# Two-block transformer on one core: rope angles on GpSimd, two more weight places, another order of small steps

## The chip, the cores and the metric

One Trainium2 chip, one core. The metric is the device time of one execution in microseconds (us), the median over runs. All data is f32. TensorE is PE in the rows, VectorE DVE, ScalarE ACT, GpSimd POOL, SyncE SP. A "q" behind a name is the engine's queue that issues a DMA.

## The reference

Two blocks of two layers each, on x of 256 tokens by 1024. Cut to what matters here:

```python
def first_block(...):
    for i in range(DEPTH):                       # DEPTH = 2
        u = h @ w_in[i]
        y_mla, y_diff, y_sb = ...                # three attentions: MLA, differential, stick-breaking
        mix = jnp.concatenate([y_mla, y_diff, y_sb], axis=-1) @ w_o[i]
        h = layer_norm(DEEPNORM_ALPHA * h + mix, ln1_g[i], ln1_b[i])
        ffn = grouped_moe(h, ...)                # 16 experts of width 512, top 2
        ple = jax.nn.sigmoid(h @ ple_gate[i]) * (p[i] @ ple_proj[i])
        h = layer_norm(DEEPNORM_ALPHA * h + ffn + ple, ln2_g[i], ln2_b[i])

def second_block(...):
    for l in range(DEPTH):
        proj = x @ w_in[l]
        a = gla_branch(...) @ w_branch[0]
        b = gmlp_branch(...) @ w_branch[1]
        c = moba_branch(...) @ w_branch[2]       # softmax attention with a partial rope
        ga, gb, gc = split(sigmoid(gl), 3)
        mix = (ga * a + gb * b + gc * c) @ w_out[l]
        x = layer_norm_2(ALPHA * x + mix, ...)
        x = layer_norm_2(ALPHA * x + jnp.square(jax.nn.relu(x @ w_ff1[l])) @ w_ff2[l], ...)
```

Rope tables are cos and sin of position times frequency, with one set of frequencies for each block.

## The kernel before, in words

**Weights.** Every large weight is cut into units of 1 MB (128 partitions by 2048 f32). `weight_plan` lists them in the order of use; SyncE loads them in that order (line 454) into numbered places, each as soon as the place's former unit has been used. A dense unit lies in one of three raw places and is split before use: ScalarE writes a rounded high part (`split_scalar`, line 461, two halves of 128x1024), VectorE the rest (`split_vector`, line 468, two halves). TensorE multiplies high by high, high by low and low by high (lines 488, 489, 492 for results with channels on partitions, 496, 499, 500 for results in rows). There are NSPLIT = 3 places for split units. The call `feed(name)` on ScalarE and on VectorE, at the point of the engine's program where it is written, splits all units up to two behind `name`; `split_scalar` first waits until TensorE has used the unit three before (`former_split`).

**Experts.** Each of the first block's layers has 96 expert units (16 experts, 6 each: gate, up, down), used whole, from 16 places: the raw and split places and parts of the arena that are free at the time. `assign_places` gives each unit the place that comes free first among those allowed; near the end of a layer fewer are allowed (the dense units that follow need theirs). Rows of tokens are picked for each expert (line 1619 multiplies them).

**Order.** Each engine runs its own program, in order, written by hand with semaphore waits. PSUM's eight banks are taken in turn (`banks.take`) or by number (`banks.hold`), each behind the engine that emptied it before.

**The first output projection.** In `block1` TensorE makes the prefix products of stick-breaking (lines 1128 to 1137), the MLA scores (line 679), turns the differential attention's rows (line 515), makes stick-breaking's y (lines 663, 664: 8 heads' products) and then runs w_o in four units of 256 rows, in the order 1, 2, 3, 0, turning MLA's probabilities and making its y between. Before these, VectorE scales the diff rows: variance (line 1436, behind ScalarE's squares of line 780), rsqrt on GpSimd (line 775), product (lines 1457, 1459); it subtracts the prefix products for stick-breaking in between (line 1451), and ScalarE takes the exponential of the result (line 1298).

**Tables.** During layer 0, steps of a generator are put between the others: the rope angles on VectorE (lines 902 to 915, 16 instructions of 128x256 for each block), sines on ScalarE (line 870), the relative bias by buckets (lines 938, 980, 878, stored and loaded again by the DMAs of lines 879 and 888, masked at line 953). GpSimd copies the up-weights (lines 1495 to 1498) and is nearly unused otherwise.

**The mix stage** of the second block: MoBA's scores (line 679) and softmax (lines 2384, 2403, 797), twelve gate units "branch gate ihj" (sigmoid at line 2158) and six branch units "branch ih", in the order gate 000, 001, 010, 011, branch 00, 01, gate 100 and so on. Behind branch 01 TensorE turns MoBA's probabilities (line 515), which ScalarE and VectorE copy (lines 2156, 809); gMLP's y is split for branch 1 (`opb_hi`, line 702, and `opb_lo`, line 705); VectorE multiplies the branch's product with the gate in two halves (line 2421).

## Time and profile before

| | us |
|---|---|
| median of 3 runs | 1705.57 (1703.49 to 1705.96) |
| the profiled execution | 1704.55 |
| its span | 1703.3 |
| TensorE busy | 1645.7 (97%) |
| VectorE busy | 890.1 (52%) |
| ScalarE busy | 716.9 (42%) |
| GpSimd busy | 33.0 (2%) |
| mean granted TensorE clock | 0.991 |
| DMA | 413.11 MB, mean 243 GB/s |

Times in the rows are in us from the span's start. A timeline row gives start, duration, engine, line, operation, what is written and read, and how many instructions run together; the brackets at its end hold the idle time before it and whose work ended it. A granted clock of 1.00 is 2.4 GHz, 0.50 is 1.2 GHz.

### The profile page before, as it was taken

Reading aid. Unit: us, or ns where it says so; the run is one execution under the profiler, and the core shown is the slowest. Engines: PE = TensorE matmul, PEld = TensorE weight load, DVE = VectorE, ACT = ScalarE, POOL = GpSimd, SP = SyncE. Lnnn points to the kernel's source line nnn. Section 1 sums busy time; section 2 is a strip of 40 time slices with the busy share of each in tenths; the row PEclk is TensorE's granted clock in tenths of the full one; section 3 lists DMA queues with packets and bytes.
Section 4 is the critical chain, followed back from the end, with each engine's and each line's share of the span. In section 5 each row is a group of like instructions: output and inputs, shape, how many; then the busy total and the mean of one; then the engine's idle time right before and its main releaser. Section 6 shows DMA issues by size and latency. Waiting matters only on the chain.

```text
span 1703.3 us, 25713 instructions
## 1 busy us (share of the span) xinstructions
PE 1645.7 (97%) x10980; PEld 1287.6 (76%) x10980; DVE 890.1 (52%) x1174; ACT 716.9 (42%) x1078; POOL 33.0 (2%) x56
## 2 busy tenths in 40 slices
PE   8899999997999999998999999999999999999998
PEld 7778644434978744433989998899889899989997
DVE  7786411113587511113568556655566675675555
ACT  4685211112575311112654543544446454354443
POOL 1000000000000000000001000000000100000000
PEclk9999999999999999998999999999999999999999
DMA  9436999997736999998744555555556355546552
GB/s 282 153 130 219 373 418 416 416 417 267 239 116 223 373 417 416 416 417 311 234 149 149 174 193 178 198 186 185 177 174 198 119 179 168 203 141 230 186 185 75
DMA packets 193111, 413.11 MB, mean 243 GB/s; under 512 B 16416, under 2 KB 130848, under 8 KB 176608
## 3 DMA queue, kind: packets, MB, share of 16 engines
q1 hardware_dynamic: 191904, 409.81, 66.8%
q10 hardware_dynamic: 1088, 1.57, 0.4%
q8 instruction: 91, 1.49, 0.4%
q14 instruction: 28, 0.23, 0.0%
HBM read 409.52 MB, written 1.84 MB: 242 GB/s over the span
## 4 chain that ended last, share of the span: by engine, by line
PE 85%; DVE 8%; DMA 4%; ACT 2%; issue 1%; POOL 0%; SPq 0%; ACTq 0%; DVEq 0%
PE PS L1619 12%; PE PS L488 10%; PE PS L492 10%; PE PS L489 10%; PE PS L496 8%; PE PS L499 8%; PE PS L500 8%; PE PS L1641 6%; DMA arena<-in_w_up 2%; DVE weights_lo L468 2%; PE PS L1653 2%; PE PS L1594 2%; PE PS L515 2%; DMA weights_raw<-in_w_in 1%; DVE hT_lo L705 1%
## 5 line engine op out<-in xcount | busy, mean ns | idle before, releaser
L468 DVE TENSOR_TENSOR weights_lo<-weights_raw,weights_hi 128x1024 fp32r<-128x1024 f32 x368 | 431.1, 1216 | 189.3 <-ACT weights_hi L461 188.8
L461 ACT ACTIVATE weights_hi<-weights_raw 128x1024 fp32r<-128x1024 f32 x368 | 365.5, 1044 | 135.3 <-PE PS L500 70.5
L488 PE MATMUL PS<-hT_hi,weights_hi 128*128 128x256 f32 (+1 forms) x1456 | 411.2, 282 | 6.1 <-ACT bias L878 2.4
L492 PE MATMUL PS<-hT_hi,weights_lo 128*128 128x256 f32 (+1 forms) x1456 | 410.0, 282 | 1.9 <-DVE weights_lo L468 1.9
L489 PE MATMUL PS<-hT_lo,weights_hi 128*128 128x256 f32 (+1 forms) x1456 | 409.1, 281 | 0.0
L488 PEld LDWEIGHTS PS<-hT_hi,weights_hi 128*128 128x128 f32 (+1 forms) x1456 | 275.1, 189 | 10.6 <-issue 5.7
L492 PEld LDWEIGHTS PS<-hT_hi,weights_lo 128*128 128x128 f32 (+1 forms) x1456 | 274.9, 189 | 3.0 <-DVE weights_lo L468 2.7
L489 PEld LDWEIGHTS PS<-hT_lo,weights_hi 128*128 128x128 f32 (+1 forms) x1456 | 275.0, 189 | 1.3
L496 PE MATMUL PS<-weights_hi,opa_hi 128*128 128x512 f32 x384 | 153.5, 400 | 0.2
L500 PE MATMUL PS<-weights_hi,opa_lo 128*128 128x512 f32 x384 | 151.6, 395 | 0.0
L499 PE MATMUL PS<-weights_lo,opa_hi 128*128 128x512 f32 x384 | 151.5, 395 | 0.0
L1878 DVE SCALAR_TENSOR_TENSOR expert_rows_lo<-PS,small,expert_rows_hi 128x512 fp32r<-128x512 f32 x32 | 24.0, 750 | 208.2 <-ACT expert_rows_hi L1743 208.2
L496 PE MATMUL PS<-weights_hi,hT_hi 128*128 128x256 f32 (+1 forms) x384 | 122.0, 318 | 8.9 <-DVE hT_lo L705 7.5
L500 PE MATMUL PS<-weights_hi,hT_lo 128*128 128x256 f32 (+1 forms) x384 | 119.9, 312 | 0.0
L499 PE MATMUL PS<-weights_lo,hT_hi 128*128 128x256 f32 (+1 forms) x384 | 119.9, 312 | 0.0
L1619 PE MATMUL PS<-weights_at_hi,picked 128*64 128x512 f32 x240 | 108.5, 595 | 2.0 <-DMA weights_at_lo<-in_w_up 2.0
L1619 PE MATMUL PS<-arena,picked 128*64 128x512 f32 x320 | 100.9, 595 | 0.0
L496 PEld LDWEIGHTS PS<-weights_hi,hT_hi 128*128 128x128 f32 x384 | 73.2, 191 | 16.5 <-DVE hT_lo L705 9.7
L500 PEld LDWEIGHTS PS<-weights_hi,opa_lo 128*128 128x128 f32 x384 | 72.1, 188 | 18.0
L496 PEld LDWEIGHTS PS<-weights_hi,opa_hi 128*128 128x128 f32 x384 | 72.2, 188 | 17.8 <-issue 1.3
L499 PEld LDWEIGHTS PS<-weights_lo,opa_hi 128*128 128x128 f32 x384 | 72.4, 188 | 15.6
L1726 ACT ACTIVATE arena<-PS 128x512 f32<-128x512 f32 x32 | 19.1, 598 | 154.1 <-PE PS L1619 154.1
(318 smaller groups left out, 2332.2 us busy)
## 6 DMA issues: line engine op xcount, KB each, us to landing
weights_raw<-in_w_in SPq DMA_DIRECT2D x80, 1024.0 KB, 5.6
weights_raw<-in_w_ff SPq DMA_DIRECT2D x64, 1024.0 KB, 5.2
arena<-in_w_down SPq DMA_DIRECT2D x28, 1024.0 KB, 20.8
arena<-in_w_up SPq DMA_DIRECT2D x22, 1024.0 KB, 13.0
weights_raw<-in_w_gate SPq DMA_DIRECT2D x20, 1024.0 KB, 16.2
arena<-in_w_gate SPq DMA_DIRECT2D x18, 1024.0 KB, 17.5
weights_at_lo<-in_w_down SPq DMA_DIRECT2D x18, 1024.0 KB, 18.2
weights_at_hi<-in_w_up SPq DMA_DIRECT2D x18, 1024.0 KB, 16.2
```

The source lines that it names most:

```text
L461: act.activation(u.flat[0][:, c:e], u.x[:, c:e], ACT.Copy).then_inc(*sig.mark("w_hi", u.u, i))
L468: dve.tensor_tensor(u.flat[1][:, c:e], u.x[:, c:e], u.flat[0][:, c:e].bitcast(F32), ALU.subtract).then_inc(*sig.mark("w_lo", u.u, i))
L488: pe.matmul(o, w[0], x[0], start=start, stop=False)
L489: pe.matmul(o, w[0], x[1], start=False, stop=False)
L492: return pe.matmul(o, w[1], x[0], start=False, stop=stop)
L496: pe.matmul(o, x[0], w[0], start=start, stop=False)
L499: pe.matmul(o, x[0], w[1], start=False, stop=False)
L500: return pe.matmul(o, x[1], w[0], start=False, stop=stop)
L515: return pe.transpose(o, i, const[0:n, C_IDENT:C_IDENT + n])
L1594: last = pe.matmul(PS[:, b, j * S:(j + 1) * S], h_split[part][:, t, 2 * kk + j, :], to_slot[:, t, :, :].rearrange("p e s -> p (e s)"), sta ...
L1619: last = pe.matmul(PS[SLOTS * j:SLOTS * j + SLOTS, b, :], x, w[j][:, k, :], start=i == k == 0, stop=i == 1 and k == 3)
L1641: last = pe.matmul(PS[SLOTS * half:SLOTS * half + SLOTS, b, :], hid_e[e_ % 2][:, 2 * i + k, :], w[:, k, 512 * half:512 * half + 512], star ...
```

## The change

- **Angles.** The second block's rope angles are computed by GpSimd, in 22 instructions of 128x256 (`angles_gpsimd`, run right behind the up-weights' copies of layer 0), and no longer by VectorE. ScalarE takes their two sines right behind the first block's two, ahead of the last bias copies.
- **Places.** Two places of their own (`unit_own`, 16 KB in each partition, which the reservation for dynamic DMA held before) are added: 18 in all. Three expert units in place of one are asked for ahead of the end of w_o, behind its first unit, now w_o 3. The last ten expert units of a layer no longer take raw places.
- **First output projection.** Stick-breaking's y stands ahead of the turning of the diff rows (now in banks 6 and 7), w_o runs in the order 3, 1, 2, 0, the diff variance stands behind stick-breaking's subtraction on VectorE, and the feeds are shifted to the new order.
- **Mix stage.** TensorE makes MoBA's scores behind the first gate unit, ScalarE and VectorE do the softmax between the first gate units, and the feed of "branch gate 100" stands on ScalarE ahead of gMLP's high part and on VectorE ahead of the two products of branch 01.

```diff
-N_EARLY, N_LATE = 3, 4
+N_FIRST, N_EARLY, N_LATE = 3, 3, 4
...
-        plan += experts[:1]
-        for i in (1, 2, 3, 0):
+        for i in (3, 1, 2, 0):
             rows(f"w_o {i}", a["w_o"][l], 256 * i)
+            if i == 3:
+                plan += experts[:N_FIRST]
         rows("ple proj", a["ple_proj"][l], 0)
         cols("ple gate 0", a["ple_gate"][l], 0)
-        plan += experts[1:1 + N_EARLY]
+        plan += experts[N_FIRST:N_FIRST + N_EARLY]
         for i in range(1, 4):
             if i == 3:
-                plan += experts[1 + N_EARLY:N_EARLY + 3]
+                plan += experts[N_FIRST + N_EARLY:N_FIRST + N_EARLY + 2]
             cols(f"ple gate {i}", a["ple_gate"][l], 256 * i)
-        plan += experts[N_EARLY + 3:-N_LATE]
+        plan += experts[N_FIRST + N_EARLY + 2:-N_LATE]
...
+        unit_own = sb("units_of_experts", [P, 2, UNIT])
...
-        N_PLACE = NRAW + 2 * NSPLIT + 7
+        N_PLACE = NRAW + 2 * NSPLIT + 9
+        AT_OWN = range(N_PLACE - 9, N_PLACE - 7)
...
+                    for i in AT_OWN:
+                        free_from[i] = -1.5
                 d = before_experts[int(name[-1])] % NSPLIT
                 allowed = [i for i in range(N_PLACE) if (left > 12 or i != AT_PARAMS) and (i != AT_ROWS or left == 6 * N_EXP) and
-                           (left > 10 or i not in (NRAW + d, NRAW + NSPLIT + d)) and
-                           (left > 12 or (i in IN_ARENA) == (left <= len(IN_ARENA)))]
+                           (left > 10 or i >= NRAW and i not in (NRAW + d, NRAW + NSPLIT + d)) and
+                           (left > 12 or i in AT_OWN or (i in IN_ARENA) == (left <= len(IN_ARENA)))]
...
-            if first:
-                for t in range(NT):
-                    banks.hold(pe, f"{label} t{t}", (4 + 2 * t, 5 + 2 * t), "dve_took")
...
+                    if not begun:
+                        banks.hold(pe, f"{label} t{t}", (4 + 2 * t, 5 + 2 * t), "dve_took")
...
-                    act.wait_ge(*sig.at("tab_dve", f"angle {blk}{part}"))
-                    act.activation(rope_tab[:, 2 * blk + part, :], red[part], ACT.Sin,
+                    act.wait_ge(*(sig.at("tab_pool", f"angle 1{part}") if blk else sig.at("tab_dve", f"angle 0{part}")))
+                    act.activation(rope_tab[:, 2 * blk + part, :], rope_tab[:, 2 + part, :] if blk else red[part], ACT.Sin,
                                    scale=col(COL_SIGN) if part else 1.0).then_inc(*sig.mark("tab_act", f"rope {blk}"))
...
                 if i == 13:
                     sines(0)
+                    sines(1)
...
-            sines(1)
...
-            take_steps(angles(1), 7)
-            yield
...
+        def angles_gpsimd(pool):
+            c = "tab_pool"
+            step(pool, c, pool.tensor_scalar(ang2, posf[:, 1, :], col(COL_INV1 + 1), None, ALU.mult))
+            for part in range(2):
+                r = rope_tab[:, 2 + part, :]
+                step(pool, c, pool.tensor_scalar(turns2, ang2, 1.0 / TWO_PI, 0.25 * (1 - part), ALU.mult, ALU.add))
+                step(pool, c, pool.tensor_scalar(turns2, turns2, MAGIC, None, ALU.add))
+                step(pool, c, pool.tensor_scalar(turns2, turns2, MAGIC, None, ALU.subtract))
+                for former, piece in ((ang2, PI1), (r, PI2), (r, PI3)):
+                    step(pool, c, pool.tensor_scalar(piece2, turns2, -piece, None, ALU.mult))
+                    step(pool, c, pool.tensor_tensor(r, former, piece2, ALU.add))
+                if part == 0:
+                    step(pool, c, pool.tensor_scalar(r, r, TWO_PI / 4, None, ALU.add))
+                step(pool, c, pool.tensor_scalar(r, r, 3.1415925, -3.1415925, ALU.min, ALU.max), f"angle 1{part}")
...
-            pe.wait_ge(*sig.at("diff_dve", n_("rows")))
-            for t in range(NT):
-                b = banks.hold(pe, n_(f"diff y{t}"), (3 + t,), "act_took")
-                for hd in range(4):
-                    last = transpose(pe, PS[:, b, hd * P:(hd + 1) * P], orow1[:, t, hd, :])
-                last.then_inc(*sig.mark("ps", n_(f"diff y{t}")))
             pe.wait_ge(*sig.at("sb_act", n_("weights")))
             b = banks.hold(pe, n_("sb y"), (3,), "act_took dve_took")
             for hd in range(4):
                 last = values_T(pe, half_rows(b, hd), sv, z, hd)
             last.then_inc(*sig.mark("ps", n_("sb y")))
-
+            pe.wait_ge(*sig.at("diff_dve", n_("rows")))
+            for t in range(NT):
+                b = banks.hold(pe, n_(f"diff y{t}"), (6 + t,), "act_took")
+                for hd in range(4):
+                    last = transpose(pe, PS[:, b, hd * P:(hd + 1) * P], orow1[:, t, hd, :])
+                last.then_inc(*sig.mark("ps", n_(f"diff y{t}")))
+
+            pe.wait_ge(*sig.at("dve_took", n_("sb y")))
+            accumulate_rows(pe, L("w_o 3"), opa, 6, n_("ln1"), True, False)
             pe.wait_ge(*sig.at("diff_dve", n_("y lo 0")))
-            accumulate_rows(pe, L("w_o 1"), opa, 2, n_("ln1"), True, False,
+            accumulate_rows(pe, L("w_o 1"), opa, 2, n_("ln1"), False, False,
                             midway=lambda: pe.wait_ge(*sig.at("diff_dve", n_("y lo 1"))))
-            accumulate_rows(pe, L("w_o 2"), opa, 4, n_("ln1"), False, False)
             turn_probs(pe, n_("mla"), M1, (0, 2), sig.at("mla_dve", n_("mla s1") + " probs"))
-            pe.wait_ge(*sig.at("dve_took", n_("sb y")))
 
             def mla_y():
                 pe.wait_ge(*sig.at("act_took", n_("mla") + " turn0"))
@@ -1169,7 +1187,7 @@
                     last = values_T(pe, half_rows(b, hd), mv, MT, hd)
                 last.then_inc(*sig.mark("ps", n_("mla y")))
 
-            accumulate_rows(pe, L("w_o 3"), opa, 6, n_("ln1"), False, False, midway=mla_y)
+            accumulate_rows(pe, L("w_o 2"), opa, 4, n_("ln1"), False, False, midway=mla_y)
...
             act.activation(z, z, ACT.Exp).then_inc(*sig.mark("sb_act", n_("weights")))
+            act.wait_ge(*sig.at("ps", n_("sb y")))
+            hi_part(act, opa[0][:, 6:8, :], one_bank(banks.of(n_("sb y")), 2)).then_inc(*sig.mark("act_took", n_("sb y")))
             for t in range(NT):
                 act.wait_ge(*sig.at("ps", n_(f"diff y{t}")))
                 step(act, "act_took", act.activation(y_raw[t], one_bank(banks.of(n_(f"diff y{t}")), 4), ACT.Copy,
                                                      scale=b1cols[:, l, 3:4]), n_(f"diff y{t}"))
                 hi_part(act, opa[0][:, 2:6, t * P:(t + 1) * P], y_raw[t]).then_inc(*sig.mark("diff_act", n_(f"y hi {t}")))
+            feed(n_("w_o 3"))
             mla_exp(0)
-            act.wait_ge(*sig.at("ps", n_("sb y")))
-            hi_part(act, opa[0][:, 6:8, :], one_bank(banks.of(n_("sb y")), 2)).then_inc(*sig.mark("act_took", n_("sb y")))
             mla_exp(1)
-            feed(n_("w_o 2"))
+            feed(n_("w_o 1"))
             act.wait_ge(*sig.at("p_in", l))
             hi_part(act, opb[0][:, 0:2, :], pT).then_inc(*sig.mark("ple_act", n_("p hi")))
             turn_takes(act, n_("mla"), 0, 0, MT, copy).then_inc(*sig.mark("act_took", n_("mla") + " turn0"))
-            feed(n_("w_o 3"))
+            feed(n_("w_o 2"))
...
-            dve.wait_ge(*sig.at("junk_act", n_("diff squares")))
-            dve.tensor_scalar(so1[:, 8:16], so1[:, 0:8], 1.0 / P, EPS_LN, ALU.mult, ALU.add).then_inc(*sig.mark(c, n_("diff var")))
...
                 dve.tensor_tensor(zi, zi, PS[:, 4 + 2 * i:6 + 2 * i, 0:384], ALU.subtract).then_inc(
                     *sig.mark("dve_took", n_("sb later")))
+            dve.wait_ge(*sig.at("junk_act", n_("diff squares")))
+            dve.tensor_scalar(so1[:, 8:16], so1[:, 0:8], 1.0 / P, EPS_LN, ALU.mult, ALU.add).then_inc(*sig.mark(c, n_("diff var")))
...
-            feed(n_("w_o 1"))
+            dve.wait_ge(*sig.at("act_took", n_("sb y")))
+            lo_part(dve, opa[1][:, 6:8, :], one_bank(banks.of(n_("sb y")), 2), opa[0][:, 6:8, :]).then_inc(
+                *sig.mark("dve_took", n_("sb y")))
             mla_max(0)
             for t in range(NT):
                 s = slice(t * P, (t + 1) * P)
                 dve.wait_ge(*sig.at("diff_act", n_(f"y hi {t}")))
                 lo_part(dve, opa[1][:, 2:6, s], y_raw[t], opa[0][:, 2:6, s]).then_inc(*sig.mark(c, n_(f"y lo {t}")))
             mla_max(1)
+            feed(n_("w_o 3"))
             mla_probs(0)
-            dve.wait_ge(*sig.at("act_took", n_("sb y")))
-            lo_part(dve, opa[1][:, 6:8, :], one_bank(banks.of(n_("sb y")), 2), opa[0][:, 6:8, :]).then_inc(
-                *sig.mark("dve_took", n_("sb y")))
             mla_probs(1)
-            feed(n_("w_o 2"))
+            feed(n_("w_o 1"))
             turn_takes(dve, n_("mla"), 2, 1, MT, copy).then_inc(*sig.mark("dve_took", n_("mla") + " turn1"))
             dve.wait_ge(*sig.at("ple_act", n_("p hi")))
             lo_part(dve, opb[1][:, 0:2, :], pT, opb[0][:, 0:2, :]).then_inc(*sig.mark("ple_dve", n_("p")))
-            feed(n_("w_o 3"))
+            feed(n_("w_o 2"))
...
+            if l == 0:
+                angles_gpsimd(pool)
...
+            def mix_scores():
+                pe.wait_ge(*sig.at("mix_dve", n_("k rope")))
+                for t in range(NT):
+                    scores(pe, n_(f"mix s{t}"), t, lambda hd, t, n: (mq[:, hd, t * P:(t + 1) * P], mk[:, hd, 0:n]))
 
             def gate_and_branch(i):
                 for half in range(2):
-                    project_T(pe, L(f"branch gate {i}{half}0", f"branch gate {i}{half}1"), hT, "act_took")
+                    for j in range(2):
+                        project_T(pe, L(f"branch gate {i}{half}{j}"), hT, "act_took")
+                        if i == half == j == 0:
+                            mix_scores()
...
+                    for j in range(2):
+                        name = n_(f"branch gate {i}{half}{j}")
+                        if not (fed and half == j == 0):
+                            feed(name)
+                        act.wait_ge(*sig.at("ps", name))
+                        through(sigT[half], ACT.Sigmoid)(PS[:, banks.of(name), :].rearrange("p (j s) -> p j s", j=2), 2 * j).then_inc(
+                            *sig.mark("act_took", name))
+                        if i == half == 0:
+                            mix_exp(j)
                 feed(*L(f"branch {i}0", f"branch {i}1"))
 
             gate_and_branch(0)
+            feed(n_("branch gate 100"))
             act.wait_ge(*sig.at("ps", n_("branch 01")))
             act.wait_ge(*sig.at("gmlp_dve", n_("y")))
             hi_part(act, opb[0][:, :, :], zT).then_inc(*sig.mark("opb_act", n_("branch 1")))
             turn_takes(act, n_("mix"), 4, 0, MTT, copy).then_inc(*sig.mark("act_took", n_("mix") + " turn0"))
-            gate_and_branch(1)
+            gate_and_branch(1, fed=True)
...
+            def gate_and_branch(i, fed=False):
+                if i == 0:
+                    feed(n_("branch gate 000"))
+                    mix_softmax(0)
+                    feed(n_("branch gate 001"))
+                    mix_softmax(1)
+                    for t in range(NT):
+                        k0, n = seg(t)
+                        softmax_scale(dve, n_(f"mix s{t}"), st_mix[t], MIX[:, :, k0:k0 + n], n, "mix_dve")
+                for half in range(i == 0, 2):
+                    feed(*L(f"branch gate {i}{half}0", f"branch gate {i}{half}1")[fed and half == 0:])
                 for half in range(2):
                     feed(n_(f"branch {i}{half}"))
+                    if (i, half) == (0, 1):
+                        feed(n_("branch gate 100"))
```

VectorE around the first output projection, layer 0; `small` holds variances, `z` and the diff rows lie in the arena. Before:

```order
L1436 TENSOR_SCALAR small<-small 128x8
L1451 TENSOR_TENSOR arena<-arena,PS 128x768 x2
L1457 SCALAR_TENSOR_TENSOR small<-small 128x8
L1459 TENSOR_TENSOR arena<-arena,small 128x1024
L468 TENSOR_TENSOR weights_lo<-weights_raw,weights_hi 128x1024 x2
L1440 TENSOR_TENSOR PS<-PS,const 64x4x64
```

and of the change:

```order
L1467 TENSOR_TENSOR arena<-arena,PS 128x768 x2
L1470 TENSOR_SCALAR small<-small 128x8
L1475 SCALAR_TENSOR_TENSOR small<-small 128x8
L1477 TENSOR_TENSOR arena<-arena,small 128x1024
L711 TENSOR_TENSOR opa_lo<-PS,opa_hi 128x512
L1456 TENSOR_TENSOR PS<-PS,const 64x4x64
```

The subtraction now stands ahead of the variance, and stick-breaking's low part (`opa_lo<-PS`) in the place of the split of a w_o unit, which comes later.

VectorE at the end of branch 01, where `L468` and `L475` are halves of split units. Before:

```order
L468 TENSOR_TENSOR weights_lo<-weights_raw,weights_hi 128x1024 x10
L2421 TENSOR_TENSOR arena<-PS,arena 128x512 x2
L468 TENSOR_TENSOR weights_lo<-weights_raw,weights_hi 128x1024 x2
L2421 TENSOR_TENSOR arena<-PS,arena 128x512 x2
L705 TENSOR_TENSOR opb_lo<-arena,opb_hi 128x1024
L809 COPY arena<-PS 128x768
```

and of the change:

```order
L475 TENSOR_TENSOR weights_lo<-weights_raw,weights_hi 128x1024 x6
L2465 TENSOR_TENSOR arena<-PS,arena 128x512 x2
L475 TENSOR_TENSOR weights_lo<-weights_raw,weights_hi 128x1024 x4
L2465 TENSOR_TENSOR arena<-PS,arena 128x512 x2
L711 TENSOR_TENSOR opb_lo<-arena,opb_hi 128x1024
L815 COPY arena<-PS 128x768
```

One more unit (two halves) is split between the products of branch 00 and those of branch 01. ScalarE at the same place, before:

```order
L461 ACTIVATE weights_hi<-weights_raw 128x1024 x4
L702 ACTIVATE opb_hi<-arena 128x1024
L2156 ACTIVATE arena<-PS 128x768
L461 ACTIVATE weights_hi<-weights_raw 128x1024 x2
L2158 ACTIVATE arena<-PS 128x512
```

and of the change:

```order
L468 ACTIVATE weights_hi<-weights_raw 128x1024 x6
L708 ACTIVATE opb_hi<-arena 128x1024
L2181 ACTIVATE arena<-PS 128x768
L2183 ACTIVATE arena<-PS 128x512
```

The unit that was split behind `arena<-PS` (the copy of the turned probabilities) is now split ahead of `opb_hi`.

## Rows read from the trace of the kernel before

**Rows 1.** The page, part 1: busy time, share of the span, instructions.
```profile
PE 1645.7 (97%) x10980; PEld 1287.6 (76%) x10980; DVE 890.1 (52%) x1174; ACT 716.9 (42%) x1078; POOL 33.0 (2%) x56
```

**Rows 2.** TensorE's waits by line: us in total, times, longest us.
```profile
PE PS L515 <- DVE arena L1459: 3.8, 2, 1.9
...
PE PS L679 <- DVE arena L2384: 3.1, 2, 1.6
...
PE PS L1619 <- DMA weights_at_lo<-in_w_up: 2.0, 2, 1.1
...
PE PS L1619 <- DMA arena<-in_w_up: 0.7, 2, 0.4
```

**Rows 3.** Timeline, 117 to 128 us: start, duration, engine, line, [idle before <-releaser].
```profile
119.17 1.82 DVE L1451 TENSOR_TENSOR arena<-arena,PS 128x768 f32<-128x768 f32 x2
...
121.02 1.48 ACT L1298 ACTIVATE arena<-arena 128x1536 f32<-128x1536 f32 x1
...
122.50 1.09 PE L515 MATMUL PS<-const,arena 128*128 128x128 f32 x8 [1.90 <-DVE arena L1459]
124.03 1.13 PE L663 MATMUL PS<-arena 128*64 128x256 f32 x4 [0.43 <-ACT arena L1301]
...
126.81 0.59 PE L496 MATMUL PS<-weights_hi,opa_hi 128*128 128x512 f32 x1
```

**Rows 4.** Windows, TensorE: us, busy (instructions), granted clock, DMA share, GB/s.
```profile
120.00:123.60 3.60, 1.70 (x11) 1.00 0.54 156
123.60:127.00 3.40, 2.97 (x17) 0.50 1.01 414
200.00:380.00 180.00, 180.00 (x1004) 1.00 1.02 416
971.00:974.60 3.60, 3.60 (x30) 1.00 0.10 13
```

**Rows 5.** Timelines of layer 0's tables, and line 888's DMAs.
```profile
28.20 0.85 POOL L1498 COPY params<-params 128x256 f32<-128x256 f32 x1
...
429.70 0.40 POOL L1498 COPY params<-params 128x256 f32<-128x256 f32 x1
...
28.72 0.61 DVE L909 SCALAR_TENSOR_TENSOR arena<-arena 128x256 f32<-128x256 f32 x1
...
31.57 0.80 PE L980 MATMUL PS<-opb_lo,steps_and_slots 128*16 128x384 f32 x2 [1.78 <-DVE opb_lo L938]
...
61.51 0.49 ACT L870 ACTIVATE rope_tab<-arena,const 128x256 f32<-128x256 f32 x1
...
L888 ACTq DMA_DIRECT2D bias<-bias_by_head x4: 326/453/455, 66.5 to 67.8; - x4
...
DMA to landing us min/median/max: 2.9/3.7/4.2
...
74.22 0.43 DVE L911 SCALAR_TENSOR_TENSOR arena<-arena 128x256 f32<-128x256 f32 x1
74.68 0.29 DVE L915 TENSOR_SCALAR arena<-arena 128x256 f32<-128x256 f32 x1
...
89.86 0.67 PE L1094 MATMUL PS<-params,arena 128*128 128x256 f32 x2 [1.22 <-ACT arena L1257]
```

**Rows 6.** Timeline, 958 to 973 us, the end of branch 01.
```profile
967.66 0.69 DVE L2421 TENSOR_TENSOR arena<-PS,arena 128x512 f32<-128x512 f32 x1 [1.58 <-PE PS L492]
968.75 1.23 DVE L705 TENSOR_TENSOR opb_lo<-arena,opb_hi 128x1024 fp32r<-128x1024 f32 x1 [0.40 <-ACT opb_hi L702]
...
967.66 1.06 ACT L702 ACTIVATE opb_hi<-arena 128x1024 fp32r<-128x1024 f32 x1 [3.63 <-PE PS L492]
...
969.31 1.99 ACT L461 ACTIVATE weights_hi<-weights_raw 128x1024 fp32r<-128x1024 f32 x2
...
967.46 0.82 PE L515 MATMUL PS<-const,arena 128*128 128x128 f32 x6
...
970.99 0.35 PE L488 MATMUL PS<-hT_hi,weights_hi 128*128 128x256 f32 x1 [1.65 <-DVE arena L809]
```

27 lines of the change are left out of this document (9 added, 18 removed).

## Prediction

> **What bounds the kernel now.** First the page: TensorE is busy 1645.7 of 1703.3 us [rows 1]. 57.6 us of idle time are therefore all that an edit of order can win, unless it makes matmuls faster or slower, and only what fills or opens a gap of TensorE counts. Next the waits by line [rows 2] name the gaps that this change touches: 3.8 us before the transposes of line 515 (twice), 3.1 us before the MoBA scores of line 679 (twice), 2.0 and 0.7 us on expert units still loading (twice each). Then timelines of the places [rows 3, 5, 6], and the windows for the granted clock [rows 4]. The DMA side has one bound: from 200 to 380 us it moves 416 GB/s at a busy share of 1.02, with TensorE busy 180.00 of 180 [rows 4]: both are full there, and neither leads by much.
>
> All sums are made against the profiled execution, 1704.55 us; the median of the runs is 1705.57, 1.0 higher. Below 0.2% (3.4 us) a measurement of this kernel can't tell a difference.
>
> **Part 1, the order before the first output projection (both layers).** Before, VectorE ends the stick-breaking weights' subtraction at about 121.0 (119.17 + 1.82), then scales the diff rows (line 1459), and TensorE, which is done with the MLA scores at 120.60, waits 1.90 us for these rows, transposes them, waits 0.43 us, and only then makes stick-breaking's y; w_o begins at 126.81 [rows 3]. TensorE's y products take 126.81 - 124.03 = 2.8 us, since the granted clock stands at 0.50 from 123.6 to 127.0, where it was 1.00 until 123.6, after 1.9 us idle [rows 4].
> The change frees VectorE of its wait on the squares before the subtraction (the order's rows below the diff have it so), so the subtraction ends with the last prefix product, about 119.0, ScalarE's exponential (1.48 us, no split in front of it) at 120.55, and stick-breaking's y can start at 120.65, just as TensorE has finished the scores. It takes about 1.5 us at full clock (half of 2.8). The diff rows come no sooner (the squares and GpSimd's rsqrt set them, 122.4), so the transposes stand at 122.45 again, but behind them only a high part (0.6) and a low part (0.65) of stick-breaking's y remain (at half the width of the 1.06 and 1.23 of [rows 6]), and these run beside them. w_o 3 starts at about 123.55 in place of 126.81: **-3.3 us**; in layer 1 by the same steps -3.1. Sum **-6.3**, bounds -4.5 (w_o 3's first matmuls still at half clock) to -7.5 (the clock does not fall at all). The banks: diff y now takes banks 6 and 7 instead of 3 and 4, free by then.
>
> **Part 2, two more places, three units asked earlier.** With 18 places the loads run up to 17 units ahead of use, in place of 15. Two units are 2 MB, at 416 GB/s 5.0 us [rows 4]. SyncE issues the two additional loads behind w_o 3 and ahead of w_o 1 and 2, where the DMA engines have room (0.54 busy from 120 to 123.6). In the steady stretch this changes nothing, as TensorE has no gap there. At its end the two waits of each layer (2.0 and 0.7 us over both layers, the longest 1.1 [rows 2]) and the 3.3 us by which part 1 brings TensorE there sooner come to 4.6 us (1.3 + 3.3), less than 5.0: at most -2.7. Against it stands the assignment of the last units: units 87 to 90 of 96 now take places given back only 6 to 7 units before, where it was 9 to 15. A load takes 2.5 us, and one asked for 6 to 7 units before its use can stand behind four others before it is late, so most of the gain stays: **-2.3**, bounds -2.7 to +1.
>
> **Part 3, the second block's rope angles to GpSimd (layer 0 only).** VectorE loses 16 instructions of 0.29 to 0.43 us that end at 74.9 (the last two stand at 74.22 and 74.68 [rows 5]). What follows them, the bias's masking, needs the bias, whose four loads were issued from 66.5 to 67.8 and took up to 4.2 us: 72.0, and ScalarE's two sines (0.8 us), now ahead of the last two bias copies, make it 72.8. VectorE's lead is 2.1 us, and TensorE can use it: it waits 1.22 us at 89.86 for ScalarE's diff values, which follow VectorE's row maxima. So **-2.1**. GpSimd's 22 instructions stand at 29 us, where VectorE is packed. What two do there: GpSimd's copy takes 0.85 us at 28.20 against 0.40 alone at 429.70, and VectorE's instruction beside it 0.61 at 28.72 against the usual 0.43 [rows 5]. 0.17 us per GpSimd instruction times 14 to 22 gives 2.4 to 3.7 us of VectorE's time; as TensorE waits 1.78 us for VectorE until 31.57, most of it reaches it: +2.4. At the other end, if each of 22 holds VectorE for its full 0.29, +6.4; below, 0. Net **+0.3**, bounds -2.1 to +4.3.
> The Trainium skill speaks against this edit (SBUF — State Buffer, Who interferes with whom): a VectorE instruction with two SBUF inputs, or in a two-port mode, and a GpSimd instruction exclude each other for a whole instruction. The 0.61 for 0.43 agrees in direction, and GpSimd's doubled copy too; by the page's rule taken fully the sum would be 4 us worse, and that is the upper bound's case.
> GpSimd is done with all of it at 29 + 22 x 0.85 = 48 us, and ScalarE, whose second sine stands at 61.51, asks at 62: nobody waits.
>
> **Part 4, MoBA's scores behind the first branch gate unit (both layers).** The wait of 1.5 us (3.1 in two [rows 2]) before the scores is covered by a whole gate unit on TensorE: **-3.1**. ScalarE now goes sigmoid, exponential, sigmoid, with more table loads (the order has 32 in place of 26); ScalarE idles 3.63 us at one point of this stretch [rows 6] and is never what TensorE waits for there, so nothing.
> The other half of the edit is the feed of "branch gate 100", moved to before the high part of gMLP's y (ScalarE) and before VectorE's two products with branch 01. A feed also splits two units further, here "branch gate 110", whose place among the three split units is that of "branch 01". So this split waits until TensorE has used branch 01, T = 967.46, and what stands behind it waits as well. Count from T: ScalarE's first half +1.0, VectorE's two halves of 1.2 (the 1.23 of the low part of the same width [rows 6]) to T + 3.45, the two products 2 x 0.7 to T + 4.8 (the second stood at 967.66 before), then low part and copy of the turned probabilities, and TensorE's gate unit 2.24 us after that low part's start (970.99 - 968.75 [rows 6]): T + 7.05, where it was 970.99 = T + 3.53. **+3.5 per layer, +7.0.** TensorE idles 5.3 us of this (1.7 are transposes). After 1.90 us idle the clock fell to 0.50 for 3.4 us, after the 1.65 us here it stayed at 1.00 [rows 3, 4]. At 0.50 a stretch of 3.4 us does 1.7 us of work; I charge 1.1 us per layer, +2.2 (0 to 1.7 each). Part 4 together **+6.1**, bounds +3.9 to +7.3.
>
> **Sum.** -6.3 - 2.3 + 0.3 + 6.1 = -2.2: 1702.35 against the profiled execution, 1703.4 against the median; I take **1703.0**. That is no measurable difference, with a tilt to faster.
>
> **Rivals.**
> (a) *The split of gate 110 hurts nobody* (0.2). For it: ScalarE splits a unit in 2.0 us and is idle 3.63 before [rows 6]; the branch products may be elsewhere than I read. Against: the order's rows put six splits before opb_hi and four before the two products. Then part 4 is -3.1 and the sum -11.4: 1694 from the median; where TensorE has half of the wait, 1699.
> (b) *GpSimd locks VectorE for good, or ScalarE waits for GpSimd* (0.2), the case on the slower side. Mechanism: 22 GpSimd instructions in VectorE's densest stretch, each excluding it; the price is 6.4 us at 0.29 each and up to 10 us where an instruction loses half of GpSimd's 0.85 [rows 5]. From a slip of 4.6 us on (2.4 + 2.2) the sum is above zero: 1705.57 - 2.2 + 4 to 8 gives 1707.4 to 1711.4. Against: the two pieces measured lost 0.17 each, and where VectorE itself waits for ScalarE the slip is swallowed. It is the case that the rule of the Trainium skill's page above (SBUF — State Buffer) describes; the trace bears it out in part.
> (c) *The tail of the experts stalls* (0.1): a unit whose place comes free only 6 units before waits for its load. Price: up to 2 us per layer and the 2.3 not won, +4 to +6 on my sum: 1707.4 to 1709.4.
> (d) *The earlier loads give nothing* (0.15): what part 1 wins before the experts, TensorE hands back waiting for DMA at the experts' end, as the transfers are the bound (416 GB/s) and their start hangs on the places, not on TensorE. Then parts 1 and 2 shrink from -8.6 to about -4: 1708.
>
> **How the numbers follow.** My reading has a chance of 0.35, its range 1699 to 1708, from the bounds of parts 3 and 4 (-2.4 and -2.2, +4.0 and +1.2, hardly all at once). With the rivals: faster by over 0.2% (under 1702.2): a little under half of my own case (0.16) and all of (a) (0.2), 0.36; slower by over 0.2% (over 1709.0): half of (b), a quarter of (c) and of (d), and what I did not see, 0.2; the rest, 0.44, is the same. The range that leaves 2 in 10 out is 1696 to 1709.5.
>
> **What would show each step.** Part 1: w_o's first matmul near 123.5, stick-breaking's y (line 663) straight behind the scores, the wait on the scaled rows shorter than 1. Part 2: no wait on a DMA at either end of the experts, or a new one among the last ten units. Part 3: the bias mask on VectorE at 72 to 73; VectorE's instructions between 29 and 50 us above their usual 0.29 and 0.43 in duration, GpSimd's 22 near 0.8. Part 4: no wait in front of the scores; in front of the gate unit behind branch 01 a wait of over 4 us for VectorE's copy, with a granted clock of 0.50 behind it. If this wait isn't there, (a) holds and the time falls below 1699; if TensorE waits more than 4 us at 30 to 60 us, (b).

## The result, and the profile after

The changed kernel takes 1707.21 us (median of 20 runs, 1704.09 to 1709.58), the kernel before 1704.53 us (20 runs, 1701.8 to 1707.27): a ratio of 1.0015, with a 95% interval of 1.0009 to 1.0021. It is slower by 2.7 us. The forecast of 1703.0 was a gain of 2.6 us on the 1705.57 that it started from. The profiled execution took 1707.19 us, its span is 1705.9.

The page of the changed kernel, busy times and the chain of waits (compare [rows 1]):

```profile
PE 1649.5 (97%) x10980; PEld 1292.6 (76%) x10980; DVE 889.5 (52%) x1158; ACT 724.4 (42%) x1084; POOL 53.8 (3%) x78
...
PE 89%; DVE 6%; ACT 2%; DMA 1%; issue 1%; POOL 0%; SPq 0%; ACTq 0%; DVEq 0%
```

TensorE is busy 3.8 us more with the same 10980 matmuls, which points to a lower clock or pace; the mean granted clock fell from 0.991 to 0.985. Its waits by line (as [rows 2]: us in total, times, longest us):

```profile
PE PS L522 <- DVE arena L2465: 9.2, 2, 4.9
...
PE PS L495 <- ACT bias L885: 3.1, 1, 3.1
...
PE PS L522 <- DVE arena L1477: 0.8, 2, 0.4
```

The waits of [rows 2] are gone or small (line 1477, the former 1459, has 0.8 in place of 3.8; those for the scores and for the experts' DMAs are missing from the list). A new one leads it: 9.2 us in two, before the transposes behind branch 01 (line 522, the former 515), for VectorE's product with the gate (line 2465, the former 2421).

Since both traces hold the same number of matmuls in nearly the same order, one can subtract the start of the n-th matmul of before from that of the changed kernel. Where this distance moves, a term is won or lost (two executions of the same code differ by some tenths of a microsecond in such a step, over the first 97 us by up to 1.0):

```
stretch (us of before)                     distance     moved
0 to 65: tables, beside GpSimd's angles     0 -> 4.0     +4.0
65 to 97: diff attention                    4.0 -> 1.2   -2.8
115 to 136: order before w_o                1.2 -> -2.2  -3.4
experts of layer 0, their end              -2.2 -> -3.2  -1.0
layer 1, order before w_o                  -3.2 -> -6.3  -3.1
experts of layer 1, their end              -6.3 -> -7.6  -1.3
end of the first block                     -7.6 -> -8.2  -0.6
MoBA's scores, layer 0                     -8.2 -> -10.2 -2.0
behind branch 01, layer 0                 -10.2 -> -3.2  +7.0
1000 to 1280                               -3.2 -> -2.1  +1.1
MoBA's scores, layer 1                     -2.1 -> -4.2  -2.0
behind branch 01, layer 1                  -4.2 -> 1.9   +6.1
1450 to the end                             1.9 -> 2.6   +0.7
```

**The order before w_o** did what it was written for. Timeline of the changed kernel, layer 0 (TensorE arrives 1.2 us late from the tables here):

```profile
119.17 0.95 DVE L1467 TENSOR_TENSOR arena<-arena,PS 128x768 f32<-128x768 f32 x1 [0.73 <-PE PS L1155]
...
120.16 1.48 ACT L1315 ACTIVATE arena<-arena 128x1536 f32<-128x1536 f32 x1
...
122.38 1.22 DVE L1477 TENSOR_TENSOR arena<-arena,small 128x1024 f32<-128x1024 f32 x1
...
121.70 0.66 PE L669 MATMUL PS<-arena 128*64 128x256 f32 x4
...
123.66 1.09 PE L522 MATMUL PS<-const,arena 128*128 128x128 f32 x8 [0.39 <-DVE arena L1477]
...
124.69 0.50 PE L503 MATMUL PS<-weights_hi,opa_hi 128*128 128x512 f32 x1
```

Stick-breaking's y (lines 669 and 670) stands right behind the scores at full clock and takes 1.6 us (121.70 to 123.66 - 0.39) where it took 2.8 [rows 3]; the wait on the scaled rows is 0.39 in place of 1.90, and w_o starts at 124.69, which is 2.1 sooner for a TensorE that came 1.2 late. The windows of the same places as in [rows 4] (us, busy, granted clock, DMA share, GB/s):

```profile
120.00:123.60 3.60, 3.27 (x25) 1.00 0.12 36
123.60:127.00 3.40, 3.34 (x18) 1.00 1.01 390
```

The clock no longer falls: 1.00 from 123.6 to 127.0, where it was 0.50.

**Behind branch 01** (T = 957.26 us, layer 0), against [rows 6]:

```profile
957.52 2.00 ACT L468 ACTIVATE weights_hi<-weights_raw 128x1024 fp32r<-128x1024 f32 x2 [3.68 <-PE PS L499]
...
958.61 2.36 DVE L475 TENSOR_TENSOR weights_lo<-weights_raw,weights_hi 128x1024 fp32r<-128x1024 f32 x2 [3.33 <-ACT weights_hi L468]
960.89 1.28 DVE L2465 TENSOR_TENSOR arena<-PS,arena 128x512 f32<-128x512 f32 x2
962.09 1.21 DVE L711 TENSOR_TENSOR opb_lo<-arena,opb_hi 128x1024 fp32r<-128x1024 f32 x1
964.55 0.96 DVE L815 COPY arena<-PS 128x768 f32<-128x768 f32 x1 [1.25 <-PE PS L522]
...
961.72 2.79 PE L522 MATMUL PS<-const,arena 128*128 128x128 f32 x12 [4.29 <-DVE arena L2465]
965.65 0.55 PE L495 MATMUL PS<-hT_hi,weights_hi 128*128 128x256 f32 x1 [1.14 <-DVE arena L815]
```

T is the moment at which TensorE has used branch 01: 957.26 is the 967.46 of before less the distance of 10.2 from the table. ScalarE splits gate 110 at 957.52, VectorE at 958.61 to 960.9, and only then come both products (x2, 1.28 us). The transposes start at 961.72, T + 4.5, where they started at T before; they take 2.79 us in place of 1.7; VectorE's copy waits 1.25 us for them, and gate 100 starts at 965.65, T + 8.4, where it was T + 3.5. The windows:

```profile
957.00:960.40 3.40, 0.43 (x4) 0.97 0.78 286
960.40:963.80 3.40, 2.08 (x10) 0.50 0.40 122
963.80:967.20 3.40, 2.26 (x11) 0.50 0.48 186
967.20:970.60 3.40, 3.40 (x18) 0.52 0.00 0
970.60:974.00 3.40, 3.40 (x31) 1.00 0.00 0
```

TensorE runs at 0.50 from 960.4 to about 970.4, so that the transposes and some 5 us of gate 100 go at half pace. Layer 1 has the same stretch:

```profile
1410.80:1421.00 10.20, 6.19 (x28) 0.50 0.30 112
```

**The angles.** Timeline of the changed kernel, GpSimd and VectorE, in layer 0:

```profile
30.94 0.46 POOL L980 TENSOR_SCALAR arena<-arena 128x256 f32<-128x256 f32 x1
31.48 0.91 POOL L981 TENSOR_SCALAR arena<-arena 128x256 f32<-128x256 f32 x1
...
37.75 1.71 POOL L984 TENSOR_SCALAR arena<-arena 128x256 f32<-128x256 f32 x1
...
37.00 3.08 DVE L475 TENSOR_TENSOR weights_lo<-weights_raw,weights_hi 128x1024 fp32r<-128x1024 f32 x2
...
47.01 1.75 DVE L943 SCALAR_TENSOR_TENSOR opb_lo<-arena,const,small 128x256 fp32r<-128x256 f32 x2
```

Beside GpSimd, VectorE's two halves of a split take 3.08 us in place of 2.35, and the two comparisons of line 943 take 1.75 in place of 1.14. GpSimd loses too, but its own durations have to be compared by the kind of instruction. In the kernel `angles_later` of experiment 5 the last three of the 22 run while VectorE does nothing:

```profile
67.51 0.85 POOL L985 TENSOR_SCALAR arena<-arena 128x256 f32<-128x256 f32 x1
68.44 0.74 POOL L986 TENSOR_TENSOR rope_tab<-rope_tab,arena 128x256 f32<-128x256 f32 x1
69.27 0.40 POOL L989 TENSOR_SCALAR rope_tab<-rope_tab 128x256 f32<-128x256 f32 x1
```

A tensor_scalar with one operation (line 985, a product) takes 0.85 us alone, one with two operations (line 989, minimum and maximum) 0.40. So the 0.46 above is the two-operation instruction of line 980, hardly slowed, and the 1.71 of line 984 is the one-operation form at twice its time.

TensorE's wait for a copy of the bias by ScalarE (3.1 us in the waits by line above) was this in the kernel before:

```profile
64.21 0.36 PE L488 MATMUL PS<-hT_hi,weights_hi 128*128 128x256 f32 x1 [2.42 <-ACT bias L878]
```

### The profile page after: what moved, and what is told of

Same layout as the page of the kernel before. It is cut to its first block, busy times and chain, and to the rows that moved or that the text cites. A ratio compares the mean times of both kernels' runs of the same rounds, so it can differ in the third digit from the quotient of the medians.

```text
span 1705.9 us, 25726 instructions
## 1 busy us (share of the span) xinstructions
PE 1649.5 (97%) x10980; PEld 1292.6 (76%) x10980; DVE 889.5 (52%) x1158; ACT 724.4 (42%) x1084; POOL 53.8 (3%) x78
## 4 chain that ended last, share of the span: by engine, by line
PE 89%; DVE 6%; ACT 2%; DMA 1%; issue 1%; POOL 0%; SPq 0%; ACTq 0%; DVEq 0%
PE PS L1639 13%; PE PS L495 11%; PE PS L499 11%; PE PS L496 11%; PE PS L503 9%; PE PS L507 8%; PE PS L506 8%; PE PS L1661 6%; PE PS L522 2%; PE PS L1673 2%; PE PS L1614 2%; DVE weights_lo L475 1%; DMA weights_raw<-in_w_in 1%; DVE h L735 1%; DVE hT_lo L711 1%
## 5 line engine op out<-in xcount | busy, mean ns | idle before, releaser
L475 DVE TENSOR_TENSOR weights_lo<-weights_raw,weights_hi 128x1024 fp32r<-128x1024 f32 x368 | 432.1, 1218 | 201.2 <-ACT weights_hi L468 200.7
L468 ACT ACTIVATE weights_hi<-weights_raw 128x1024 fp32r<-128x1024 f32 x368 | 365.7, 1045 | 131.8 <-PE PS L507 66.6
L1639 PE MATMUL PS<-weights_at_lo,picked 128*64 128x512 f32 x192 | 86.9, 595 | 0.0
L506 PEld LDWEIGHTS PS<-weights_lo,opa_hi 128*128 128x128 f32 x384 | 72.2, 188 | 16.3
```

What stands on the lines that cost most here:

```text
L468: act.activation(u.flat[0][:, c:e], u.x[:, c:e], ACT.Copy).then_inc(*sig.mark("w_hi", u.u, i))
L475: dve.tensor_tensor(u.flat[1][:, c:e], u.x[:, c:e], u.flat[0][:, c:e].bitcast(F32), ALU.subtract).then_inc(*sig.mark("w_lo", u.u, i))
L506: pe.matmul(o, x[0], w[1], start=False, stop=False)
L1639: last = pe.matmul(PS[SLOTS * j:SLOTS * j + SLOTS, b, :], x, w[j][:, k, :], start=i == k == 0, stop=i == 1 and k == 3)
```

## The experiments

All times are medians; the kernel before ran beside them with 1704.59 (late_gate, products_first, clock_kept, angles_back), 1705.28 (gate_only, clock_kept_less, late_gate_angles_back, angles_later) and 1705.68 us (places_undone, places_only, scores_back). Intervals are of the ratio to it, and reach about 2 us to either side; so a difference of 1 us between two medians is read only together with their traces.

**1. The early feed put back (late_gate).** The part of the change suspected first, undone alone.

```diff
             gate_and_branch(0)
-            feed(n_("branch gate 100"))
...
-                    if (i, half) == (0, 1):
-                        feed(n_("branch gate 100"))
...
-            gate_and_branch(1, fed=True)
+            gate_and_branch(1)
```

> The changed kernel with one thing put back: the feed of branch gate 100 stands where it stood before, on ScalarE and VectorE. Theory A (the early split of gate 110 holds back everything behind branch 01 and then the clock falls: 7.0 us in layer 0 and 6.1 in layer 1 by the traces): the 4.3 us wait before the transposes behind branch 01 is gone, the granted clock stays at 1.00 there, and the time is 1707.2 - 13 = 1694, 10 below the kernel before. Theory B (MoBA's scores between the gate units, with their table switches on ScalarE, are what disturbs the stage): the wait shrinks but the time stays within 3 us of 1707.

Measured: 1692.7 us, ratio 0.9927 (0.9914 to 0.9941): 14.5 us below the changed kernel and 11.9 below the one before. In its trace the unit behind branch 01 starts where it did before the change, T + 3.5:

```profile
960.05 0.36 PE L495 MATMUL PS<-hT_hi,weights_hi 128*128 128x256 f32 x1 [1.65 <-DVE arena L815]
```

and the distance between this trace and that of the changed kernel moves by -7.0 us here in layer 0, -6.9 in layer 1, and in no other stretch of the table by more than 0.8. Theory A stands. The scores between the gates do no harm.

**2. VectorE's products ahead of the split (products_first).** Which queue makes the loss?

```diff
-                    if (i, half) == (0, 1):
-                        feed(n_("branch gate 100"))
...
                             dve.tensor_tensor(m, m, s, ALU.add).then_inc(*sig.mark("merge_dve", n_(f"merged {i} {half}{c}")))
+                    if (i, half) == (0, 1):
+                        feed(n_("branch gate 100"))
```

> The changed kernel, with VectorE's part of the early feed moved behind its two products of branch 01 (ScalarE's part stays). Theory A (VectorE's products stand in the queue behind the split, and they free the bank for the transposes): transposes start right behind branch 01 at full clock; then low part and copy still wait for the split, gate 100 starts at about T + 5.6 in place of T + 8.4, and the clock falls for a shorter time: 3.5 us less per layer, 1700. Theory B (ScalarE's high part, behind the split, is what counts): no more than 1 us is won.

Measured: 1700.07 us, ratio 0.9972 (0.9959 to 0.9984), 7.1 below the changed kernel. TensorE behind branch 01:

```profile
957.44 0.82 PE L522 MATMUL PS<-const,arena 128*128 128x128 f32 x6
958.47 0.84 PE L522 MATMUL PS<-const,arena 128*128 128x128 f32 x6 [0.22 <-DVE arena L2463]
963.30 0.36 PE L495 MATMUL PS<-hT_hi,weights_hi 128*128 128x256 f32 x1 [3.98 <-DVE arena L815]
```

The transposes run right behind branch 01, at full clock, as before; the gate unit starts at T + 5.9 (T = 957.4), behind low part and copy, which the split still holds. The clock falls here too, but behind the gate unit's start only and for a third of the time:

```profile
963.60:967.00 3.40, 3.40 (x18) 0.51 0.57 223
967.00:970.40 3.40, 3.40 (x31) 1.00 0.00 0
```

So half of the 14.5 us comes from the two products standing behind the split (7.1), and half (7.4) is left when only they are put ahead of it: low part and copy behind the split, and this shorter fall of the clock. Theory A stands, theory B does not.

**3. The clock kept up in the wait (clock_kept, clock_kept_less).** TensorE is given matmuls that compute nothing used, in the wait behind branch 01: 36 calls, and in a second kernel 17.

```diff
             gate_and_branch(0)
+            keep_clock(pe, banks.turn % 8, 36)
             turn_probs(pe, n_("mix"), MIX, (4, 6), sig.at("mix_dve", n_("mix s1") + " probs"))
```

> The changed kernel with 36 more small matmuls (128x128, into the bank that gate 100 takes next, overwritten) in TensorE's wait behind branch 01, in both layers. They compute nothing that is used. Theory A1 (5 us of my 7 are waiting, 2.2 the halved clock afterwards, and the transposes at half clock add 1.3 to the wait): the granted clock stays at 1.00, and the time falls by 2 x 3.4 = 7 us, to 1700. Theory A2 (the wait alone makes the loss): 1707, unchanged.

Measured: 1705.95 us, ratio 1.0011 (1.0002 to 1.002), 1.3 below the changed kernel; neither expectation. The trace shows why: each call is two matmuls, and 72 of them take 8.2 us, which ends 3.7 us after the bank for the transposes is free:

```profile
956.36 8.20 PE L518 MATMUL PS<-const 128*128 128x128 f32 x72
...
964.39 1.47 PE L522 MATMUL PS<-const,arena 128*128 128x128 f32 x12
...
967.01 0.36 PE L495 MATMUL PS<-hT_hi,weights_hi 128*128 128x256 f32 x1 [1.14 <-DVE arena L815]
```

The dose was wrong, and the clock's gain paid for it. With 17 calls:

> The changed kernel with 17 unused matmuls in TensorE's wait behind branch 01, some 3.9 us of them, so that they end before the transposes may start (36 calls took 8.2 us and reached 3.6 us past that point). Theory A1 (the halved clock costs 2.2 us behind gate 100 and 1.3 in the transposes, per layer): 1707.2 - 6.5 = 1700.7. Theory A2 (the clock's part is small): above 1705.

Measured: 1700.81 us, ratio 0.9973 (0.9962 to 0.9984), 6.4 below the changed kernel.

```profile
956.78 3.96 PE L518 MATMUL PS<-const 128*128 128x128 f32 x34
961.24 1.50 PE L522 MATMUL PS<-const,arena 128*128 128x128 f32 x12 [0.50 <-DVE arena L2466]
963.88 0.36 PE L495 MATMUL PS<-hT_hi,weights_hi 128*128 128x256 f32 x1 [1.14 <-DVE arena L815]
```

The transposes take 1.50 us in place of 2.79, the gate unit starts at T + 7.1, and the windows from 960.4 and 963.8 us show the clock:

```profile
960.40:963.80 3.40, 1.84 (x16) 1.00 0.58 189
963.80:967.20 3.40, 3.32 (x28) 1.00 0.33 125
```

So of the loss of 14.5 us, 6.4 (7.2 by the two ratios to the kernel before) is the halved clock, in the transposes and behind (theory A1); the rest is waiting for the split. With the clock kept, T + 7.1 is just what the prediction had worked out for the gate unit.

**4. The early feed alone (gate_only).** The kernel before with this one edit, as in the diff of the change.

> The kernel before with nothing but the early feed of branch gate 100, on ScalarE and VectorE. Theory A (the early split is a loss by itself, whatever stands around it): the wait of 4.3 us before the transposes and the halved clock behind them appear here too, 7.0 us in layer 0 and 6 to 7 in layer 1: 1704.6 + 13.5 = 1718. Rival (it costs only together with the scores between the gate units): under 1708.

Measured: 1718.88 us, ratio 1.0075 (1.0061 to 1.0089): +13.6. Its wait has the length of that of the changed kernel:

```profile
PE PS L515 <- DVE arena L2429: 9.2, 2, 4.9
```

The edit costs the same with and without the others (13.6 and 14.5, closer than the intervals can tell apart).

**5. The angles (angles_back, late_gate_angles_back, angles_later).** First the angles on VectorE again, in the changed kernel and in that with the late feed.

```diff
                     sines(0)
-                    sines(1)
...
+            sines(1)
...
+            take_steps(angles(1), 7)
+            yield
...
-            if l == 0:
-                angles_gpsimd(pool)
```

> The changed kernel with the second block's rope angles on VectorE again, and ScalarE's sines at their former place. Theory C (GpSimd costs VectorE 2.6 us between 30 and 52 us, the sines 0.7, and 2.8 are won behind: net +0.5): 1707 or 0.5 less, with VectorE's instructions between 30 and 50 us at 0.29 and 0.43 again. Rival (GpSimd's work costs net 3 to 4 us and the rest of what the first 60 us lost comes from it too): 1703 to 1704.

Measured: 1704.37 us, ratio 0.9995 (0.9985 to 1.0004), 2.8 below the changed kernel, between the two expectations.

> The late feed of branch gate 100 and the angles on VectorE together: of the change only the order before the first output projection, the two places and the scores between the gate units stay. Theory C (the angles on GpSimd cost 2.8 us net in all that follows, as the medians of the one without them say): 1692.7 - 2.8 = 1690. Rival (they cost 1.2, as the two traces' distance behind this stage says, and the rest was chance): 1691.5.

Measured: 1691.74 us, ratio 0.9923 (0.991 to 0.9935), 1.0 below the one with GpSimd's angles, as the rival expectation had it. The two pairs give 2.8 and 1.0; behind the diff attention the traces lie 1.2 and 1.1 us apart. So the stage costs about 1.2, and what the first pair has beyond it came later and is not of this stage.

Then the same work in another place: GpSimd starts it behind VectorE's comparison number 11, and ScalarE takes the sines behind the bias's copies, as before the change.

```diff
         def angles_gpsimd(pool):
             c = "tab_pool"
+            pool.wait_ge(*sig.at("tab_dve", "past 11"))
...
                     sines(0)
-                    sines(1)
...
                     *sig.landing("bias_in", "all"))
             yield
+            sines(1)
```

> The kernel with the late feed, GpSimd's angles started behind VectorE's comparison number 11 (at about 50 us in place of 30), and their two sines at the former place behind the bias's copies. Theory C (GpSimd beside VectorE's densest stretch costs 3.3 us there, and the two early sines 0.7): VectorE is slack from 50 to 60 us, GpSimd's instructions shorten to about 0.5 us, TensorE reaches the transposes at 60 us at the old time, and VectorE's lead of 2.1 us behind it stays: 1692.7 - 4 = 1688.7, below the one with the angles on VectorE. Rival (GpSimd now ends after 65 us and holds up the MLA rsqrt of 67 us, or locks VectorE as much there): 1691 to 1693.

Measured: 1689.66 us, ratio 0.9905 (0.9891 to 0.992): the fastest kernel of the study, 3.0 below the one with the late feed alone and 2.1 below the one with the angles on VectorE. All thirteen traces agree on this stage: at one matmul behind the diff attention (number 598) the five with the angles on VectorE stand 0.5 to 0.0 us ahead of the kernel before, the five with GpSimd at 30 us stand 0.4 to 1.2 behind it, the three with GpSimd at 48 us 1.7 to 2.8 ahead. By the means of the three groups that is 1.0 lost and 2.0 won. The win is that of two changes made together, GpSimd's later start and the sines' former place; they were not separated. GpSimd from 47.67 us on, and VectorE's split where GpSimd is now idle:

```profile
47.67 0.94 POOL L978 TENSOR_SCALAR arena<-arena,const 128x256 f32<-128x256 f32 x1 [17.93 <-DVE opb_lo L943]
48.69 0.41 POOL L981 TENSOR_SCALAR arena<-arena 128x256 f32<-128x256 f32 x1
49.18 1.71 POOL L982 TENSOR_SCALAR arena<-arena 128x256 f32<-128x256 f32 x1
...
34.75 2.36 DVE L475 TENSOR_TENSOR weights_lo<-weights_raw,weights_hi 128x1024 fp32r<-128x1024 f32 x2
```

VectorE's split is back at 2.36. GpSimd's instructions did not shorten as expected (0.41 to 1.71 again). What the rival expectation feared did happen in part: GpSimd is done with the angles only at 69.7, its rsqrt for the MLA rows stands behind them, and VectorE waits 4.01 us for it, where it waited 1.13 before:

```profile
70.83 0.32 DVE L1388 TENSOR_SCALAR arena<-arena,small 128x192 f32<-128x192 f32 x1 [4.01 <-POOL small L781]
...
71.69 0.75 DVE L956 TENSOR_TENSOR bias<-bias,const 64x256 f32<-64x256 f32 x2
```

The bias's masking behind it (line 956) stands at 71.69 all the same, where it was at 74.89 before the change, as the 16 instructions that VectorE no longer has are worth more than this wait.

**6. The places (places_undone, places_only).** The fastest kernel with 16 places and one early unit, and the kernel before with the two places and three early units alone.

```diff
-N_FIRST, N_EARLY, N_LATE = 3, 3, 4
+N_FIRST, N_EARLY, N_LATE = 1, 3, 4
...
-        N_PLACE = NRAW + 2 * NSPLIT + 9
-        AT_OWN = range(N_PLACE - 9, N_PLACE - 7)
+        N_PLACE = NRAW + 2 * NSPLIT + 7
```

> The fastest kernel so far (late feed, GpSimd's angles later) with 16 places again and one expert unit asked for behind w_o 3. Theory P (the places are worth the two waits on a DMA, 1.2 us per layer, and nothing else, because the loads of the arena's places start as much sooner as TensorE does): 1689.7 + 2.4 = 1692. Rival (without them the experts' end is set by the DMA, so that TensorE hands back the 3.3 us won before w_o as well): waits of up to 4.6 us per layer, 1697 to 1699.

Measured: 1692.79 us, ratio 0.993 (0.9917 to 0.9942): 3.1 more than with the places. TensorE's list has one wait on an expert unit's DMA, in one layer, not 1.2 us in each as theory P had it:

```profile
PE PS L1634 <- DMA weights_at_lo<-in_w_up: 2.7, 1, 2.7
```

> The kernel before with the two places and three early units alone (behind w_o 1, its first). Theory P: the two waits on a DMA of each layer go, 1.1 and 1.3 us: 1705 - 2.4 = 1702.5. Rival (the two places only matter once the order before w_o brings TensorE there sooner): 1704.5 to 1705.

Measured: 1701.96 us, ratio 0.9982 (0.9974 to 0.9991): 3.7 less than before, 1.3 more than expected. Its TensorE has no wait on an expert unit's DMA left. The sum of theory P stands on both sides, with both rivals outside; rival (d) of the prediction, the gain before w_o handed back at the experts' end, would have shown as 7 to 9 us in the first of them.

**7. The scores (scores_back).** The fastest kernel with MoBA's scores and softmax ahead of the gates.

```diff
-                        if i == half == j == 0:
-                            mix_scores()
...
+            mix_scores()
             gate_and_branch(0)
```

(On ScalarE and VectorE the exponentials and the rest of the softmax likewise.)

> The fastest kernel so far with MoBA's scores and softmax ahead of the branch gates again, as before. The theory (a wait of 1.55 us per layer is covered, and about 0.5 more by the traces' distance): 1689.7 + 4.0 = 1693.7. Rival (the softmax between the gates costs ScalarE and VectorE as much as it covers): below 1691.

Measured: 1693.45 us, ratio 0.9931 (0.9919 to 0.9943): 3.8 us more, so the edit is worth 3.8.

## Why the prediction was wrong

Point by point, in its own steps:

- **Part 1, the order before w_o: right.** Forecast -6.3 (its terms, -3.3 and -3.1, make -6.4), by the traces -3.4 and -3.1, -6.5. w_o starts at 124.69 with TensorE 1.2 us late, for 123.55 forecast on time; the clock does not fall behind it, with a wait of 0.39 in place of 1.90. This edit was not undone by itself; but the step of -3.39 in layer 0 and -3.10 in layer 1 stands, to 0.01 us, at the same matmuls in all ten traces that have the edit, and is missing (0.3 us or less) in the two new ones that don't, gate_only and places_only.
- **Part 2, the places: right.** Forecast -2.3, -2.3 by the traces, 3.1 and 3.7 us won by the medians. The tail (rival c) never stalled.
- **Part 3, the angles: sign right, size off.** Forecast +0.3, about +1.2 measured (1.0 by the means of all traces). The slip was 3.3 us by the angles put back (TensorE's matmul number 300 stands at 47.63 us there, at 50.95 in the changed kernel), in the range that was worked out from the two copies (2.4 to 3.7), of which the low end was taken. The step that failed is the net: the two early sines add 0.7 on ScalarE's path of bias copies; it was counted against VectorE's lead alone, while TensorE itself waits there. TensorE's one wait for such a copy is 3.1 us, where it was 2.42 (both rows above). GpSimd was done with the 22 at 52.4 us, for 48 forecast, and still long before ScalarE asked. The rule of the Trainium skill (SBUF — State Buffer, Who interferes with whom) has two-input and two-port instructions of VectorE and an instruction of GpSimd exclude each other for a whole instruction, whoever starts first; the 3.08 for 2.35 and the 1.75 for 1.14 agree in kind. In size each of GpSimd's 22 instructions took 0.15 us of VectorE on average, not a whole one of 0.29, so the upper bound of 6.4 us was not reached.
- **Part 4, the scores: better than forecast.** -3.1 forecast, -4.0 by the traces, -3.8 by undoing them.
- **Part 4, the early feed: the mechanism right, the size wrong, and this turned the result.** Forecast +7.0 and +2.2 for the clock, 9.2 in all, with an upper bound of 10.4; measured 13.1 by the traces (13.9 between the changed kernel and the late feed), 14.5 and 13.6 by the medians. The wait is what was forecast: 3.5 us per layer to T + 7.05, and T + 7.1 with the clock kept. The step that failed is the clock's price, in two places. "T + 7.05" took the transposes to run beside VectorE's low part; they start at T + 4.5, at half clock they take 2.8 us, and so they end after the low part, and the copy waits for them: T + 8.4. And the clock was charged for after the gate unit's start only, with 1.1 us per layer, from a stretch at 0.50 of 3.4 us [rows 4]; it was down for 10.2 us in each layer, the transposes included, and experiment 3 puts its price at 3.2 us per layer: 6.4 in place of the +2.2 in the sum. Without this slip the sum would have been above zero.
- **The sum.** With the terms by the traces (-6.5, -2.3, +1.2, -4.0, +13.1, and -0.6 at the end of the first block, which the forecast did not have) it would be +0.9. The rest, 1.8 us, is the two stretches from 1000 us on; in the first of them TensorE starts a matmul every 0.119 us in place of 0.117 (medians) at the same granted clock. Part of that is not the change's doing, since places_only, which has none of the edits behind 1000 us, goes at 0.119 there as well, and late_gate, which has them all but the early feed, at 0.117. But the medians of twenty runs of each kernel lie 2.7 apart as the two traces do, so it is not shown that the rest is chance alone. With the 14.5 us that undoing the early feed gave, in place of 13.1, the sum is +2.3, and 0.4 stays open.

Of the rivals, (a), that the split of gate 110 hurts nobody, is what the late feed shows one would have had without it. (b), the case on the slower side, had the right direction by luck, as the time rose by another cause: what GpSimd's angles cost net is a tenth of what the early feed lost.

## What to carry to other kernels

A call that looks ahead ("prepare two more") waits for whatever its furthest unit needs; before moving such a call forward in an engine's program, write down what the new last unit waits for, and which short instructions now stand behind it. Here three edits worth 13 us hid under one that cost 14, and only undoing them one at a time showed it: a change of five parts that comes out near zero should be taken apart. Work moved to an idle engine should be placed where the engine that it slows has slack, not as early as its inputs allow: the same 22 instructions cost 1.0 us at 30 us and, with the two sines back in their place, won 2.0 at 48. And an idle time of TensorE is to be priced with the matmuls behind it at half clock, the ones inside the wait's own chain too.

## What the runs showed of the hardware

- TensorE at a granted clock of 1.00 does not always keep the same pace. From 1020 to 1240 us the matmuls of 128x256 start at a median of 0.117 us after each other in five traces (before, late_gate, products_first, clock_kept, angles_back) and of 0.119 in eight (the changed kernel and the seven experiments of the second and third group, whatever they change); the means are 117.5 and 118.6 ns. Over this stretch that makes 0.7 to 1.1 us, about as much as two runs of one kernel differ.
- After 4.3 us without a matmul, and then the transposes and another short wait, the granted clock stood at 0.50 for 10.2 us (from 960.4), in which TensorE was itself waiting part of the time. With the transposes done first and 3.98 us without a matmul behind them it stood at 0.50 for 3.4 us (products_first, from 963.6). With the wait filled up to 0.50 us before the transposes it stayed at 1.00.
- GpSimd's tensor_scalar of 128x256 in f32 took 0.85 us with one operation and 0.40 with two, each with VectorE idle; tensor_tensor took 0.74. Beside VectorE the one-operation form took up to 1.71. Summed over the 22, GpSimd took 20.8 us in place of the 16.3 that these durations give (an estimate), 0.20 us lost for each; VectorE lost 0.15 for each.
